# Attention in a TensorE-bound encoder: from a looped order to one straight order by heads, with maxima reduced in pairs

## The chip, the cores and the metric

The kernel runs on one core of a Trainium2 chip. TensorE does the matrix products, VectorE (DVE) and ScalarE (ACT) work on their results in PSUM, GpSimd (POOL) works on tiles in SBUF, and SyncE (SP) issues the DMAs. The engines run side by side and wait for each other through semaphores. The metric is the time on the device in microseconds, median of three runs.

## The reference

A two-layer encoder is applied to two groups of tokens, 2048 "prompt" tokens and 512 "sample" tokens, which attend only within their group. The change is in the attention of layer 0, 12 heads of width 96 for queries and keys and 64 for values:

```python
def one_block(qblk):
    s = jnp.einsum('bqhd,bkhd->bhqk', qblk, k, preferred_element_type=jnp.float32) * scale
    p = jax.nn.softmax(s, axis=-1)
    return jnp.einsum('bhqk,bkhd->bqhd', p.astype(v.dtype), v)
```

All numbers are float32. The rest (latents, head projections, memory attention, spatial gating, gates and output products) is the same in both kernels.

## The kernel before

Each float32 operand is kept as a high part in fp32r and a low part, and a product is made of several fp32r matmuls. The attention stage (`attention`, from line 937) works in chunks. A chunk is one head and 512 queries. A prompt chunk has 8 pairs of 128-key tiles (2048 keys), a sample chunk 2 pairs (512 keys). There are 48 prompt chunks and 12 sample chunks, all prompt chunks first.

For each pair t of a chunk the engines do this:

- TensorE, `scores`: six matmuls of 512 columns (two key tiles, three products each) into `sc[t % 2]`, two PSUM banks. It needs the remainder of pair t-2 (`p_lo`), which is read from the same banks, and for t = 0 the row of negated maxima of the chunk, which rides along as the 97th row of the query tile.
- ScalarE, `exps`: exp of the scores into `ph` (fp32r, L1193), and again in place (L1194).
- VectorE, `low_of`: the remainder `pl` = exact minus rounded (L1301).
- TensorE, `value`: four matmuls with `ph` and `pl` into `o_hi` and `o_lo`, two pairs behind the scores.
- GpSimd: the running sum `acc` of `ph` (L1267).
- TensorE, `maximum`, and VectorE, `maxima`: a rough product of queries and keys for a chunk further on, 16 pieces a prompt chunk, 4 a sample chunk, two pieces in each unit. A piece is one matmul into one bank (`mxp0` or `mxp1`) and one reduction by VectorE (L1287). When all pieces of a chunk are there, VectorE reduces them to four columns (`m4`, L1290) and negates them (`neg`, L1295), and SyncE copies them by four small DMAs into the query tile (`row`, L1036).

What TensorE and VectorE do for one t is called a unit here: in a full one 12 matmuls. At a chunk's end come: ScalarE's copies of the upper half and the low rows (`upper`), VectorE's `halves` (L1306, one per chunk), GpSimd's `fold`, `total_lo` and `join`, and two TensorE matmuls for the sum (`total`). The last two value products of a chunk are issued in unit 0 of the next one (`finish_values`).

The order on each engine is that of the code. `run_chunks` writes 8 chunks out, then a hardware loop of 4 passes over 8 chunks, then the other 20 chunks written out. In unit t TensorE's `step` does scores t+1, the maxima, the scores 0 of the next chunk where t is the last, then the value products. The maxima of a prompt chunk are made from 10 units ahead (`max_pieces`), those of a sample chunk two short chunks ahead.

Of the kernel before, what the change touches and what calls it, by code (L numbers as in the profile page):

```python
# [6 lines left out]
ALU = mybir.AluOpType  # L7
# [865 lines left out]
class Chunk:  # L873
# [3 lines left out]
    PROMPTS, LAST = NH * PROMPT // BLK, NH * (PROMPT + SAMPLE) // BLK - 1  # L877

    def __init__(self, j, k):
        if isinstance(j, int):  # L880
            j, k = (8 * j + k) // 8, (8 * j + k) % 8
        self.j, self.k = j, k
        self.known = isinstance(j, int)
        m = 8 * j + k - self.PROMPTS if self.known else -1
        self.sample = m >= 0
        self.pairs = 2 if self.sample else 8
        self.pieces = 4 if self.sample else 16
        p = self.PROMPTS
        self.n = j * 8 + k
        self.slot = k % 2  # L890
        self.quad = k % 4
        self.part = k % 4
        self.load = j * 2 + k // 4
        self.kv = (k // 4) % 2
        self.g0 = p * 8 + 2 * m if self.sample else j * 64 + 8 * k
        self.sum0 = p * 7 + m if self.sample else j * 56 + 7 * k
        self.mx0 = p * 16 + 4 * m if self.sample else j * 128 + 16 * k
        self.g0_mod = (2 * m) % 4 if self.sample else 0
        self.half = j * 4 + k // 2
        self.tile0 = 4 * self.part if self.sample else 0  # L900
# [1375 lines left out]
```

## Time and profile before

| | |
|---|---|
| median of three runs | 3671.3 us (3663.44 to 3674.0) |
| the profiled execution | 3671.86 us, its span 3670.1 us |
| TensorE clock granted, mean | 0.946 |
| busy in the span: TensorE, VectorE, ScalarE, GpSimd | 3348.8, 2017.9, 1582.6, 1389.7 us |

The attention stage lies between about 495 us and 1810 us of the span. A timeline row has start, duration, engine, line, operation, output and inputs; `x2` merges instructions of one kind, and the bracket is the idle time before it with what ended it. In a window row the count of instructions stands in parentheses behind each engine's busy time. A chunk's period can be read from any row that comes once a chunk, as that of `halves`.

### The profile page before, as it was taken

To read this page: it belongs to the slowest core of one execution; us is meant where nothing else is said; L and a number is where in the kernel's file an instruction comes from. 1 tells how busy PE (TensorE), PEld (TensorE's weight loads), DVE (VectorE), ACT (ScalarE), POOL (GpSimd) and SP (SyncE) were. 2 spreads that over 40 slices of the span, in tenths; PEclk is the share of its full clock that TensorE was granted. 3 is DMA by queue.
4 is the path that set the end of the run, shared out by engine and by line. 5 is a ranking of instruction groups with operands and counts; after the bars stand their busy time and mean duration, and the time that the engine had idled before them with its cause. 6 is when DMAs were issued, how large, how long until landed. Compare 5 with 4: busy or idle time off the path is not lost. (4 is left out here: it accounts for less than half of the span.)

```text
span 3670.1 us, 48958 instructions
## 1 busy us (share of the span) xinstructions
PE 3348.8 (91%) x16108; PEld 2745.4 (75%) x16108; DVE 2017.9 (55%) x3007; ACT 1582.6 (43%) x2396; POOL 1389.7 (38%) x914
## 2 busy tenths in 40 slices
PE   8969969999999999998779898997999969799899
PEld 7968847776776767776578687885888858688787
DVE  4457768888887878886557333113332337622211
ACT  4446637776776767776545222002222225412100
POOL 1147838887887878887511000000000011000000
PEclk9979979999999999998889899998999979899999
DMA  7769961222122212224243897655222245398555
GB/s 279 257 232 311 315 179 40 53 51 53 32 52 52 53 47 53 53 53 97 84 169 121 253 293 241 205 186 185 87 94 94 91 157 185 121 266 238 177 187 172
DMA packets 457298, 538.22 MB, mean 147 GB/s; under 512 B 55705, under 2 KB 372505, under 8 KB 437393
## 3 DMA queue, kind: packets, MB, share of 16 engines
q1 hardware_dynamic: 457104, 535.81, 47.6%
q8 instruction: 101, 1.65, 0.2%
q14 instruction: 93, 0.75, 0.1%
HBM read 324.98 MB, written 210.61 MB: 146 GB/s over the span
## 5 line engine op out<-in xcount | busy, mean ns | idle before, releaser
L1267 POOL TENSOR_TENSOR at_acc<-at_acc,at_ph 128x1024 f32<-128x1024 f32 x288 | 690.4, 2397 | 84.6 <-ACT at_ph L1193 70.2
L1301 DVE TENSOR_TENSOR at_pl<-at_sc,at_ph 128x1024 fp32r<-128x1024 f32 x408 | 498.0, 1221 | 184.4 <-ACT at_sc L1194 162.1
L1193 ACT ACTIVATE at_ph<-at_sc 128x1024 fp32r<-128x1024 f32 x408 | 418.8, 1027 | 398.1 <-PE at_sc L1113 397.7
L1287 DVE TENSOR_REDUCE at_mx<-at_mxp 128x1 f32<-128x512 f32 x816 | 521.8, 680 | 31.7 <-PE at_mxp L1124 29.0
L1194 ACT ACTIVATE at_sc<-at_sc 128x1024 f32<-128x1024 f32 x408 | 416.3, 1020 | 0.0
L1109 PE MATMUL at_sc<-at_qt,at_kt 97*128 97x512 f32 x816 | 337.7, 414 | 53.4 <-DMA at_qt<-at_neg 26.0
L1111 PE MATMUL at_sc<-at_qt,at_kt 96*128 96x512 f32 x816 | 330.1, 405 | 0.0
L1113 PE MATMUL at_sc<-at_qt,at_kt 96*128 96x512 f32 x816 | 329.1, 403 | 0.0
L1138 PE MATMUL at_o_hi<-at_ph,at_v 128*128 128x512 f32 x816 | 325.0, 398 | 1.5 <-DVE at_half L1306 1.5
L1140 PE MATMUL at_o_lo<-at_pl,at_v 128*97 128x512 f32 x816 | 323.4, 396 | 0.0
L1124 PE MATMUL at_mxp<-at_kt,at_qt 96*128 96x512 f32 x816 | 279.5, 415 | 29.6 <-DMA at_kt<-kT 23.0
L165 PE MATMUL ga_acc<-ga_h,ga_g_hi 128*128 128x512 f32 x640 | 256.8, 401 | 29.2 <-DMA ga_h<-hT 27.1
L165 PE MATMUL ou_acc<-ou_o_hi,ou_o 128*128 128x512 f32 x640 | 250.8, 392 | 26.2 <-DMA ou_o<-ogT 26.2
L1931 DVE TENSOR_TENSOR ou_y<-ou_acc,ou_x 128x1024 f32<-128x1024 f32 x40 | 49.0, 1224 | 381.4 <-PE ou_acc L167 381.4
L166 PE MATMUL ga_acc<-ga_h,ga_g_hi 128*128 128x512 f32 x640 | 254.0, 397 | 0.0
L167 PE MATMUL ga_acc<-ga_h,ga_g_lo 128*128 128x512 f32 x640 | 253.7, 396 | 0.0
L166 PE MATMUL ou_acc<-ou_o_lo,ou_o 128*128 128x512 f32 x640 | 250.4, 391 | 0.0
L167 PE MATMUL ou_acc<-ou_o_hi,ou_o 128*128 128x512 f32 x640 | 250.3, 391 | 0.0
L1109 PEld LDWEIGHTS at_sc<-at_qt,at_kt 97*128 97x128 f32 x816 | 156.9, 192 | 123.8 <-DVE at_pl L1301 31.3
L1124 PEld LDWEIGHTS at_mxp<-at_kt,at_qt 96*128 96x128 f32 x816 | 157.3, 193 | 96.4 <-DVE at_mx L1287 40.6
L253 POOL TENSOR_TENSOR sg_n_mse<-sg_n_ms,all_eps 128x1 f32<-128x1 f32 x24 | 5.0, 209 | 560.4 <-ACT sg_n_junk L245 560.4
L1267 POOL TENSOR_TENSOR at_acc<-at_ph 128x1024 f32<-128x1024 f32 x60 | 143.8, 2397 | 170.9 <-ACT at_ph L1193 170.8
(246 smaller groups left out, 7412.3 us busy)
## 6 DMA issues: line engine op xcount, KB each, us to landing
ma_h<-hT SPq DMA_DIRECT2D x40, 1024.0 KB, 4.8
ogT<-ga_st SPq DMA_DIRECT2D x160, 256.0 KB, 3.5
ou_o<-ogT SPq DMA_DIRECT2D x40, 1024.0 KB, 6.1
ga_h<-hT SPq DMA_DIRECT2D x64, 512.0 KB, 7.3
hT<-lat_n_h SPq DMA_DIRECT2D x24, 1024.0 KB, 6.3
hT<-sg_n_h SPq DMA_DIRECT2D x24, 1024.0 KB, 3.8
qT<-hd_stq SPq DMA_DIRECT2D x60, 384.0 KB, 6.0
kT<-hd_stk SPq DMA_DIRECT2D x120, 192.0 KB, 3.5
```

The lines of the kernel that those rows point to most:

```text
L165: pe.matmul(out, a_hi, w_hi, start=first, stop=False)
L166: pe.matmul(out, a_hi, w_lo, start=False, stop=False)
L167: return pe.matmul(out, a_lo, w_hi, start=False, stop=last)
L1109: pe.matmul(sc[g][:, b, :], kt[:, c.kv, 0, ks], qt[:, c.quad, 0, :], start=True, stop=False)
L1111: pe.matmul(sc[g][:, b, :], kt[0:QK, c.kv, 0, ks], qt[0:QK, c.quad, 1, :], start=False, stop=False)
L1113: m = pe.matmul(sc[g][:, b, :], kt[0:QK, c.kv, 1, ks], qt[0:QK, c.quad, 0, :], start=False, stop=True)
L1124: pe.matmul(mxp[n % 2][:], qt[0:QK, c.quad, 0, qn * P:(qn + 1) * P], kt[0:QK, c.kv, 0, kb * BLK:(kb + 1) * BLK], start=True, stop=True).th ...
L1193: act.activation(ph[:, g], sc[g % 2][:], ACT.Exp, scale=SCALE).then_inc(p_hi, 1)
L1194: act.activation(sc[g % 2][:], sc[g % 2][:], ACT.Exp, scale=SCALE).then_inc(p_in, 1)
L1267: pool.tensor_tensor(acc[:, c.slot, :], f32(ph[:, (g - 1) % 4]).rearrange("p b n -> p (b n)") if t == 1 else acc[:, c.slot, :], now, ALU.a ...
L1287: dve.tensor_reduce(mx[:, n:n + 1], mxp[n % 2][:], AX.X, ALU.max).then_inc(mx_in, 1)
L1301: dve.tensor_tensor(pl[:, g], sc[g % 2][:], f32(ph[:, g]), ALU.subtract).then_inc(p_lo, 1)
```

## The change

All 60 chunks are written out straight, without a hardware loop, in the order of the heads: four prompt chunks of a head and then its sample chunk. A head's keys and values are loaded whole, for both groups, the keys' high and low part by a DMA each with a semaphore of its own. The maxima run a fixed 11 units (22 pieces) ahead over all chunk boundaries. Two maximum matmuls write the two banks of one tile `mxp`, and one reduction takes both. The next pair may be written only when that reduction is done. For the first pieces, when the score buffers are still empty, `sc` serves as a ring. In a unit TensorE now does scores, value products, maxima. On the other engines the order within a unit is the same. `unit` and `free_of_sum` only find the semaphore values.

```diff
-    PROMPTS, LAST = NH * PROMPT // BLK, NH * (PROMPT + SAMPLE) // BLK - 1
-
-    def __init__(self, j, k):
-        if isinstance(j, int):
-            j, k = (8 * j + k) // 8, (8 * j + k) % 8
-        self.j, self.k = j, k
-        self.known = isinstance(j, int)
-        m = 8 * j + k - self.PROMPTS if self.known else -1
-        self.sample = m >= 0
+    PARTS = TOK // BLK
+    COUNT = NH * PARTS
+    UNITS, ADDS, PIECES = 34, 29, 68
+    LEAD = 22
...
+        self.slot, self.quad, self.kv = n % 2, n % 4, self.head % 2
+        self.half, self.turn = n // 2, n // 4
+        self.g0 = self.head * self.UNITS + 8 * self.part
+        self.sum0 = self.head * self.ADDS + 7 * self.part
+        self.mx0 = self.head * self.PIECES + 16 * self.part
+        self.tile0 = PT_TILES if self.sample else 0
...
+def unit(g):
+
+    head, rest = g // Chunk.UNITS, g % Chunk.UNITS
+    c = Chunk(head * Chunk.PARTS + min(rest // 8, Chunk.PARTS - 1))
+    return c, g - c.g0
 
 
 def run_chunks(eng, step):
 
-    for k in range(8):
-        step(Chunk(0, k))
-    with eng.Fori(1, Chunk.PROMPTS // 8 - 1) as j:
-        for k in range(8):
-            step(Chunk(j, k))
-    for n in range(Chunk.PROMPTS - 8, Chunk.LAST + 1):
-        step(Chunk(0, n))
+    for n in range(Chunk.COUNT):
+        step(Chunk(n))
...
-    if c.pairs == 2:
-        ahead, pieces = c.ahead(2), (2 * t, 2 * t + 1)
-    elif t < 5:
-        ahead, pieces = c.ahead(1), (2 * t + 6, 2 * t + 7)
-    else:
-        ahead, pieces = c.ahead(2), (2 * t - 10, 2 * t - 9)
-    return ahead, [n for n in pieces if ahead.exists() and n < ahead.pieces]
+    at = 2 * (c.g0 + t) + Chunk.LEAD
+    head, rest = at // Chunk.PIECES, at % Chunk.PIECES
+    ahead = Chunk(head * Chunk.PARTS + min(rest // 16, Chunk.PARTS - 1))
+    return ahead, [at - ahead.mx0, at - ahead.mx0 + 1] if ahead.exists() else []
...
-        kt = s.sb("kt", [QK + 1, 2, 2, PROMPT], F32R)
+        kt = s.sb("kt", [QK + 1, 2, 2, TOK], F32R)
         qt = s.sb("qt", [QK + 1, 4, 2, BLK], F32R)
-        v = s.sb("v", [P, 2, 16, VR + 1], F32R)
+        v = s.sb("v", [P, 2, TILES, VR + 1], F32R)
...
-        mxp = [s.ps(f"mxp{u}", [P, BLK]) for u in range(2)]
+        mxp = s.ps("mxp", [P, 2, BLK])
...
+        def max_buffer(pair):
+
+            return sc[pair % 2] if pair < 8 or pair == 9 else mxp
+
+        def max_free(pair):
+
+            return pair - 1 if pair < 8 else {8: 0, 9: 8, 10: 9}.get(pair, pair)
...
+                def load_k(head):
+                    for a, sem in ((0, kh_load), (1, kl_load)):
+                        sp.dma_start(f32(kt[0:QK, head % 2, a]), kT[a, head * QK:(head + 1) * QK, :]
+                                     ).then_inc(sem[head % 2], 16)
+
+                def load_v(head):
+                    sp.dma_start(f32(v[:, head % 2, :, 0:2 * VH]),
+                                 vS[:, head * (2 * VH):(head + 1) * (2 * VH)].rearrange("(t p) n -> p t n", p=P)
+                                 ).then_inc(v_load[head % 2], 16)
...
-                load_k(0, 0)
+                load_k(0)
                 load_q(c0.ahead(1))
-                load_v(0, 0)
+                load_v(0)
                 load_q(c0.ahead(2))
-                load_k(1, 1)
-                load_v(1, 1)
-                sp.wait_ge(const_in, 4)
+                load_k(1)
+                load_v(1)
+                sp.wait_ge(const_in, 5)
...
-                    more = not c.known or (c.load >= 1 and c.load + 1 < SLOTS)
-                    if c.part == 0 and more:
+                    if c.part == 0 and 1 <= c.head < NH - 1:
                         sp.wait_ge(scored, c.g0)
-                        load_k(c.load + 1, 1 - c.kv)
-                    if c.part == 1 and more:
-                        sp.wait_ge(valued, prev.g0)
-                        load_v(c.load + 1, 1 - c.kv)
-                    if c.sample and nxt.exists():
+                        load_k(c.head + 1)
+                    if c.part == 1 and 1 <= c.head < NH - 1:
+                        sp.wait_ge(valued, c.head * c.UNITS)
+                        load_v(c.head + 1)
+                    early = c.sample or nxt.sample
+                    if early and nxt.exists():
                         row(nxt)
                     if has_before(c):
-                        store(prev)
-                    if not c.sample and nxt.exists():
+                        store(before(c, 1))
+                    if not early and nxt.exists():
                         row(nxt)
...
-                    g = (c.g0_mod + t) % 2
+                        if c.part == 0:
+                            pe.wait_ge(kl_load[c.kv], loaded(c))
+                    g = (c.g0 + t) % 2
+                    if c.n == 0 and t < 2:
+                        pe.wait_ge(mx_in, 7 if t == 0 else 10)
                     after(pe, p_lo, c.g0 + (t - 1))
...
                     for n in pieces:
                         if n == 0:
-                            pe.wait_ge(q_load[c.quad], c.load * 16 + 16)
-                            pe.wait_ge(k_load[c.kv], loaded(c, 2))
-                        after(pe, mx_in, c.mx0 + (n - 1))
+                            pe.wait_ge(q_load[c.quad], c.turn * 16 + 16)
+                            pe.wait_ge(kh_load[c.kv], loaded(c))
+                        pair = (c.mx0 + n) // 2
+                        if n % 2 == 0:
+                            after(pe, mx_in, max_free(pair))
                         qn, kb = (n, c.part) if c.sample else (n // 4, n % 4)
-                        pe.matmul(mxp[n % 2][:], qt[0:QK, c.quad, 0, qn * P:(qn + 1) * P],
-                                  kt[0:QK, c.kv, 0, kb * BLK:(kb + 1) * BLK], start=True,
-                                  stop=True).then_inc(mx_mm, 1)
+                        m = pe.matmul(max_buffer(pair)[:, n % 2], qt[0:QK, c.quad, 0, qn * P:(qn + 1) * P],
+                                      kt[0:QK, c.kv, 0, kb * BLK:(kb + 1) * BLK], start=True, stop=True)
+                        if n % 2 == 1:
+                            m.then_inc(mx_mm, 1)
...
                     for t in range(c.pairs):
                         if t < c.pairs - 1:
                             scores(c, t + 1)
-                        maximum(*max_pieces(c, t))
                         if nxt.exists() and t == c.pairs - 1:
                             scores(nxt, 0)
                         if t == 0 and has_before(c):
                            value(c, t - 2)
                        if t == 3 and has_before(c):
                            total(prev)
+                        maximum(*max_pieces(c, t))
...
             def _(dve):
                 def maxima(c, pieces):
-                    for n in pieces:
-                        dve.wait_ge(mx_mm, c.mx0 + (n + 1))
-                        dve.tensor_reduce(mx[:, n:n + 1], mxp[n % 2][:], AX.X, ALU.max).then_inc(mx_in, 1)
+                    for n in pieces[::2]:
+                        dve.wait_ge(mx_mm, (c.mx0 + n) // 2 + 1)
+                        dve.tensor_reduce(mx[:, n:n + 2], max_buffer((c.mx0 + n) // 2)[:], AX.X, ALU.max).then_inc(mx_in, 1)
                     if len(pieces) and pieces[-1] == c.pieces - 1:
-                        dve.wait_ge(mx_in, c.mx0 + c.pieces)
+                        dve.wait_ge(mx_in, (c.mx0 + c.pieces) // 2)
```

TensorE, unit 0 of the second chunk, before: the end of scores 1, the two maximum matmuls, the eight value matmuls left from the first chunk, the first of scores 2.

```order
L1113 MATMUL at_sc1<-at_qt,at_kt 128x512
L1124 MATMUL at_mxp0<-at_kt,at_qt 128x512
L1124 MATMUL at_mxp1<-at_kt,at_qt 128x512
L1138 MATMUL at_o_hi<-at_ph,at_v 128x512
L1140 MATMUL at_o_lo<-at_pl,at_v 97x512
L1138 MATMUL at_o_hi<-at_ph,at_v 128x512
L1140 MATMUL at_o_lo<-at_pl,at_v 97x512
L1138 MATMUL at_o_hi<-at_ph,at_v 128x512
L1140 MATMUL at_o_lo<-at_pl,at_v 97x512
L1138 MATMUL at_o_hi<-at_ph,at_v 128x512
L1140 MATMUL at_o_lo<-at_pl,at_v 97x512
L1109 MATMUL at_sc0<-at_qt,at_kt 128x512
```

TensorE, the same unit in the changed kernel:

```order
L1091 MATMUL at_sc1<-at_qt,at_kt 128x512
L1119 MATMUL at_o_hi<-at_ph,at_v 128x512
L1121 MATMUL at_o_lo<-at_pl,at_v 97x512
L1119 MATMUL at_o_hi<-at_ph,at_v 128x512
L1121 MATMUL at_o_lo<-at_pl,at_v 97x512
L1119 MATMUL at_o_hi<-at_ph,at_v 128x512
L1121 MATMUL at_o_lo<-at_pl,at_v 97x512
L1119 MATMUL at_o_hi<-at_ph,at_v 128x512
L1121 MATMUL at_o_lo<-at_pl,at_v 97x512
L1104 MATMUL at_mxp<-at_kt,at_qt 128x512 x2
L1087 MATMUL at_sc0<-at_qt,at_kt 128x512
```

The two maximum matmuls stood ahead of the eight value matmuls and stand behind them now, right ahead of the next scores.

VectorE, units 3 and 4 of the same chunk, before (`at_pl` is the remainder, `at_m4` and `at_neg` the four maxima and their negation):

```order
L1301 TENSOR_TENSOR at_pl<-at_sc1,at_ph 128x1024
L1287 TENSOR_REDUCE at_mx<-at_mxp0 128x1
L1287 TENSOR_REDUCE at_mx<-at_mxp1 128x1
L1301 TENSOR_TENSOR at_pl<-at_sc0,at_ph 128x1024
L1287 TENSOR_REDUCE at_mx<-at_mxp0 128x1
L1287 TENSOR_REDUCE at_mx<-at_mxp1 128x1
L1290 TENSOR_REDUCE at_m4<-at_mx 128x4
L1295 TENSOR_SCALAR at_neg<-at_m4 128x4
L1301 TENSOR_TENSOR at_pl<-at_sc1,at_ph 128x1024
```

VectorE, the same place in the changed kernel:

```order
L1282 TENSOR_TENSOR at_pl<-at_sc1,at_ph 128x1024
L1268 TENSOR_REDUCE at_mx<-at_mxp 128x2
L1282 TENSOR_TENSOR at_pl<-at_sc0,at_ph 128x1024
L1268 TENSOR_REDUCE at_mx<-at_mxp 128x2
L1271 TENSOR_REDUCE at_m4<-at_mx 128x4
L1276 TENSOR_SCALAR at_neg<-at_m4 128x4
L1282 TENSOR_TENSOR at_pl<-at_sc1,at_ph 128x1024
```

The reductions of one piece each have become one of two pieces. Their place between the remainders, and that of the negation ahead of a remainder, is the same.

SyncE's issues at the start of the stage, before (down to the first row copies):

```order
L1007 DMA at_qt<-qT 96x2x512
L1018 DMA at_kt<-kT 96x2x2048
L1007 DMA at_qt<-qT 96x2x512
L1029 DMA at_v<-vS 128x16x128
L1007 DMA at_qt<-qT 96x2x512
L1018 DMA at_kt<-kT 96x2x2048
L1029 DMA at_v<-vS 128x16x128
L1036 DMA at_qt<-at_neg 1x128x1 x4
```

And in the changed kernel:

```order
L1000 DMA at_qt<-qT 96x2x512
L1006 DMA at_kt<-kT 96x2560 x2
L1000 DMA at_qt<-qT 96x2x512
L1010 DMA at_v<-vS 128x20x128
L1000 DMA at_qt<-qT 96x2x512
L1006 DMA at_kt<-kT 96x2560 x2
L1010 DMA at_v<-vS 128x20x128
L1017 DMA at_qt<-at_neg 1x128x1 x4
```

The key load is two DMAs, keys and values have 2560 tokens in place of 2048, and all of them stand ahead of the first row copies as before.

## Rows read from the trace of the kernel before

**Rows 1.** Windows: us, busy us (instructions) by engine, clock, DMA share, GB/s.

```profile
core 0: us, PE busy (x) PEld busy (x) DVE busy (x) ACT busy (x) POOL busy (x), PEclk, DMA share, GB/s
498.00:522.00 24.00, 11.96 (x18) 5.10 (x18) 13.93 (x24) 0.00 (x0) 0.00 (x0) 0.50 1.07 242
1540.00:1640.00 100.00, 99.57 (x420) 76.37 (x419) 88.85 (x117) 72.74 (x81) 87.83 (x44) 1.00 0.22 50
```

**Rows 2.** Groups, attention stage: count, busy us, mean ns, idle before and its releasers.

```profile
L1109 PE MATMUL at_sc<-at_qt,at_kt 97*128 97x512 f32 x816 | 337.7, 414 | 53.4 <-DMA at_qt<-at_neg 26.0 <-issue 19.9 <-DVE at_pl L1301 3.7
```

**Rows 3.** Timeline, VectorE's halves: start us, us, instruction, [idle before <-releaser].

```profile
581.79 0.67 DVE L1306 TENSOR_TENSOR at_half<-at_o_hi,at_up 64x512 f32<-64x512 f32 x1
...
605.24 0.67 DVE L1306 TENSOR_TENSOR at_half<-at_o_hi,at_up 64x512 f32<-64x512 f32 x1
...
888.24 0.67 DVE L1306 TENSOR_TENSOR at_half<-at_o_hi,at_up 64x512 f32<-64x512 f32 x1
...
921.74 0.68 DVE L1306 TENSOR_TENSOR at_half<-at_o_hi,at_up 64x512 f32<-64x512 f32 x1 [1.24 <-ACT at_up L1202]
...
1693.45 0.67 DVE L1306 TENSOR_TENSOR at_half<-at_o_hi,at_up 64x512 f32<-64x512 f32 x1
...
1804.95 0.68 DVE L1306 TENSOR_TENSOR at_half<-at_o_hi,at_up 64x512 f32<-64x512 f32 x1 [4.12 <-ACT at_up L1202]
```

**Rows 4.** Timeline around a chunk boundary in straight code, all engines.

```profile
580.80 0.40 PE L1109 MATMUL at_sc<-at_qt,at_kt 97*128 97x512 f32 x1
...
582.20 0.62 PE L1124 MATMUL at_mxp<-at_kt,at_qt 96*128 96x512 f32 x2
...
582.40 1.02 ACT L1193 ACTIVATE at_ph<-at_sc 128x1024 fp32r<-128x1024 f32 x1 [0.20 <-PE at_sc L1113]
...
584.37 1.22 DVE L1301 TENSOR_TENSOR at_pl<-at_sc,at_ph 128x1024 fp32r<-128x1024 f32 x1 [0.45 <-ACT at_sc L1194]
...
585.51 1.28 DVE L1287 TENSOR_REDUCE at_mx<-at_mxp 128x1 f32<-128x512 f32 x2
...
585.65 0.50 PE L1109 MATMUL at_sc<-at_qt,at_kt 97*128 97x512 f32 x1
...
590.40 0.63 PE L1124 MATMUL at_mxp<-at_kt,at_qt 96*128 96x512 f32 x2
...
590.84 1.29 DVE L1287 TENSOR_REDUCE at_mx<-at_mxp 128x1 f32<-128x512 f32 x2 [0.28 <-PE at_mxp L1124]
```

**Rows 5.** Timeline, VectorE's negation beside GpSimd, and the wait behind it.

```profile
543.84 2.38 POOL L1267 TENSOR_TENSOR at_acc<-at_acc,at_ph 128x1024 f32<-128x1024 f32 x1 [0.39 <-ACT at_ph L1193]
...
544.57 1.68 DVE L1295 TENSOR_SCALAR at_neg<-at_m 128x4 fp32r<-128x4 f32 x1
...
546.16 1.21 DVE L1301 TENSOR_TENSOR at_pl<-at_sc,at_ph 128x1024 fp32r<-128x1024 f32 x1
...
547.43 0.50 PE L1109 MATMUL at_sc<-at_qt,at_kt 97*128 97x512 f32 x1 [0.54 <-DVE at_pl L1301]
...
567.39 1.29 DVE L1287 TENSOR_REDUCE at_mx<-at_mxp 128x1 f32<-128x512 f32 x2 [0.28 <-PE at_mxp L1124]
...
568.92 0.78 DVE L1295 TENSOR_SCALAR at_neg<-at_m 128x4 fp32r<-128x4 f32 x1
```

**Rows 6.** Timeline, GpSimd after that same boundary.

```profile
583.50 2.39 POOL L1267 TENSOR_TENSOR at_acc<-at_acc,at_ph 128x1024 f32<-128x1024 f32 x1 [1.32 <-ACT at_ph L1193]
...
590.72 4.94 POOL L1267 TENSOR_TENSOR at_acc<-at_acc,at_ph 128x1024 f32<-128x1024 f32 x2
```

**Rows 7.** Timeline, start of the attention stage.

```profile
508.27 1.19 PE L1124 MATMUL at_mxp<-at_kt,at_qt 96*128 96x512 f32 x2 [23.04 <-DMA at_kt<-kT]
...
526.90 0.79 PE L1109 MATMUL at_sc<-at_qt,at_kt 97*128 97x512 f32 x1 [1.42 <-DMA at_qt<-at_neg]
```

**Rows 8.** Timeline, a row copy issued behind a key load.

```profile
1687.48 2.43 SPq L1036 DMA_DIRECT2D at_qt<-at_neg  x4
...
1696.26 0.79 PE L1109 MATMUL at_sc<-at_qt,at_kt 97*128 97x512 f32 x1 [3.16 <-DMA at_qt<-at_neg]
```

More of the change, by code:

```diff
@@ L898, in __init__ @@
-        self.g0_mod = (2 * m) % 4 if self.sample else 0
-        self.half = j * 4 + k // 2
-        self.tile0 = 4 * self.part if self.sample else 0
+        self.slot, self.quad, self.kv = n % 2, n % 4, self.head % 2
[4 more added lines that the diff above has]
+        self.tile0 = PT_TILES if self.sample else 0
+        self.after_sample = n > 0 and self.part == 0
@@ L969, in attention @@
         q_load = [s.sem(f"q_load{u}") for u in range(4)]
-        k_load = [s.sem(f"k_load{u}") for u in range(2)]
+        kh_load = [s.sem(f"kh_load{u}") for u in range(2)]
+        kl_load = [s.sem(f"kl_load{u}") for u in range(2)]
         v_load = [s.sem(f"v_load{u}") for u in range(2)]
@@ L973, in attention, with loaded @@
         o_out = [s.sem(f"o_out{u}") for u in range(2)]
-        SLOTS = NH + NH * SAMPLE // PROMPT
-        def loaded(c, parts):
-            if not c.sample:
-                return c.j * 16 + 16
-            return NH // 2 * 16 + ((c.load - NH) // 2 + 1) * 16 * parts
+        def loaded(c):
+            return (c.head // 2 + 1) * 16
         def stored(c):
@@ L1021, in load_v @@
[L1021 to L1031 removed]
+                    sp.dma_start(f32(qt[0:QK, c.quad]),
+                                 qT[c.head, :, :, c.part * BLK:(c.part + 1) * BLK].rearrange("a d t -> d a t")
+                                 ).then_inc(q_load[c.quad], 16)
@@ L1040, in sum_rows @@
                 def sum_rows(c, which):
-                    if c.sample:
-                        h = c.n - c.PROMPTS
-                        return sums_out[which, h:h + 1, PROMPT:TOK]
-                    return sums_out[which, bass.ds(c.load, 1), c.part * BLK:(c.part + 1) * BLK]
+                    return sums_out[which, c.head:c.head + 1, c.part * BLK:(c.part + 1) * BLK]
                 def store(c):
@@ L1150, in total @@
                     m.then_inc(tot_mm, 1)
-                pe.wait_ge(const_in, 4)
-                c0 = Chunk(0, 0)
+                pe.wait_ge(const_in, 5)
+                c0 = Chunk(0)
                 maximum(c0, range(c0.pieces))
-                maximum(c0.ahead(1), range(6))
+                maximum(c0.ahead(1), range(Chunk.LEAD - 16))
                 scores(c0, 0)
@@ L1312, in _ @@
                 dve.memset(f32(pick[:, ROW_HI:ROW_HI + 1]), 1.0).then_inc(const_in, 1)
-                maxima(Chunk(0, 0), range(16))
-                maxima(Chunk(0, 1), range(6))
+                maxima(Chunk(0), range(16))
+                maxima(Chunk(1), range(Chunk.LEAD - 16))
                 def step(c):
@@ L1323, in _ @@
                 run_chunks(dve, step)
-                halves(Chunk(0, Chunk.LAST))
+                halves(Chunk(Chunk.COUNT - 1))
 class MemoryRows:
```

93 lines of the change are left out of this document (27 added, 66 removed).

## The prediction

> **What bounds the kernel now.** I read the windows first. In the stretch of straight attention code TensorE issues 420 matmuls in 100 us at clock 1.00, while VectorE and GpSimd are each busy 88 us [rows 1]: TensorE is the bound there, with two engines close behind it. The timeline gives its pace: six score matmuls start in 1.40 us, 0.233 each [rows 4]. A prompt chunk is 98 matmuls (48 scores, 32 value, 16 maximum, 2 for the total), 22.8 us, and takes 23.45 [rows 3]. So a chunk has 0.6 us of stalls and no more. The scores group is one of six of 816 matmuls [rows 2]; with the 120 of the totals attention has 5,016.
>
> The idle time lies elsewhere. The halves, one a chunk, are a clock for progress. Over the loop's jump back they stand 33.50 us apart in place of 23.45 [rows 3]; the idle time put down to "issue" is 19.9 us [rows 2], in three places, and about as much again is given to the cold clock and refilling: 29 us in all. The twelve sample chunks take 111.5 us (1693.45 to 1804.95) for 12 x 26 matmuls, 72.7 us: 39 us lost, most of it the waits for the row of negated maxima, 26.0 us [rows 2, 3].
>
> From the first scores to the last value products the stage takes 526.90 to 1804, 1277 us [rows 3, 7]. Of it 4,992 matmuls x 0.233 are 1163.
>
> **What the change removes.** The jumps (29 us). The loop's address code: some 0.15 us a chunk over 32 chunks, 5 us. The sample tail (39 us): a sample chunk now stands between prompt chunks, and its row is ready many units before its scores. The small stalls of a chunk, 0.6 us, go too, but only to make room for others. If that were all, attention would shorten by over 70 us.
>
> **What it adds, in a full unit.** The maximum matmuls now stand last in a unit, two banks are reduced by one instruction, and VectorE's order is as before: remainder of scores t, then the reduction of unit t, then remainder t+1. TensorE may write scores t+3 only when remainder t+1 is done. Links of the chain, all from [rows 4]: maximum matmul to reduction 0.44, for a pair one matmul later, 0.67. The pair's reduction reads 1024 elements a partition, as the remainder does, so I take the remainder's pace of 1.14 (584.37 to 585.51). Two single ones in a row take 1.28, so the bounds are 1.06 and 1.36. Remainder to scores 1.28. Sum 3.09 us from the first maximum matmul. TensorE reaches those scores 14 matmuls after it, 3.26 us. Slack 0.17: nothing is lost, but before, with the maxima four matmuls earlier, there was about 0.9 us more.
>
> **At a chunk's start.** Unit 0 has the previous chunk's eight value matmuls, now ahead of its maxima; unit 1 has no value products. From unit 0's maxima to scores 3 are only 10 matmuls (its own two, scores 2, unit 1's maxima), 2.33 us, against the chain of 3.09. Stall 0.76, and scores that come late show 0.50 in place of 0.40 for the first matmul [rows 4], so 0.86. This holds at prompt and sample boundaries alike (between sample and prompt 18 matmuls stand where 16 do, ahead of the maxima, not behind). 57 of 59 boundaries still have maxima: 49 us.
>
> **At the negation.** Once a chunk VectorE also reduces the maxima to four and negates them: from the start of the two reductions to the negation 1.53 us, 1.46 with a pair, the negation 0.78, and the remainder starts 0.09 before its end [rows 5]. The chain is 0.67 + 1.46 + 0.78 - 0.09 + 1.28 = 4.10 against 3.26: 0.84, with the late start 0.94 a chunk. Before, the earlier maxima covered it.
>
> **The negation's own length.** It is 0.78 us in one row and 1.68 in the other. In the second it starts at 544.57 and ends at 546.25, where GpSimd's addition (543.84 + 2.38 = 546.22) ends; TensorE's scores then waited 0.54 [rows 5]. In each of some two dozen that I looked at with GpSimd at work, the negation ended with a GpSimd instruction. So its length is set by GpSimd's phase. That phase in the changed kernel, with the start of scores 2 as zero: first exponential 1.60, addition 1.10 later (582.40 to 583.50), and 7.22 us of additions, remainder of the total and join until the fourth addition (583.50 to 590.72) [rows 4, 6]. It starts at 9.9; the fifth runs from 12.4 to 14.8. TensorE: scores 3 at 2.62 (the stall above), scores 4 at 5.52, scores 5 at 8.78 (the total's two matmuls lie between), the maxima behind them at 11.1, the negation at 11.1 + 0.67 + 1.46 = 13.2. It falls well inside the fifth addition and ends with it at 14.8: 1.6 in place of 0.78, so the stall is 0.94 + 0.84 = 1.78. Three chunks of each head negate there: 36 x 1.78 = 64 us. The other two (for the sample chunk and for the next head) negate two units later; the same working gives 0.8 and 1.2: 23 x 1.0 = 23.
>
> The Trainium skill, SBUF — State Buffer, section Who interferes with whom, says that VectorE and GpSimd share a port pair as an exclusive lock, that a tensor_scalar can need it and a tensor_reduce on trn2 never does. By that rule the pair's reduction doesn't wait for GpSimd and the negation does; the trace agrees (1.68 against 0.78). It speaks against this change, since with it the wait lies on TensorE's path.
>
> **The start.** The first maxima start at 508.27, the first scores 18.6 us later [rows 7]. One pair per reduction and two score buffers as a ring save some 2 us, and waiting for only the high half of the keys some 3. Against it: ahead of the first row copy stand 7,552 KB of loads, before 6,272. At 242 GB/s [rows 1] that is 5.4 us more, and a row copy issued behind a key load landed only 8.8 us after its issue (1687.48 to 1696.26) [rows 8]. Bounds -5 and +5.4. I take +3, since the loads end after the row is ready by 10 us or more, which is the case of rows 8.
>
> **Sum.** 1163 matmuls, 3 for the cold start, 4 for the tail (4.12 of idle time at 1804.95 [rows 3]), 49 for the boundaries, 64 + 23 for negations: 1306 us against 1277, +29. With the start +3: +32. The profiled execution took 3671.9 (span 3670.1), 0.6 over the median: 3704. The other stages are untouched; neither DMA totals nor ScalarE's work changes.
>
> **Rivals.** *TensorE stays the bound, faster.* If the reductions don't hold up the scores (the chain shorter by some 0.8 us, or a cover that I overlook at the boundaries), 1163 + 7 + 60 x 0.6 = 1206, with +3 at the start 3604. For it: in the trace it is at 1.00 clock and 99.6 us of 100 [rows 1]. Against it: the four links are measured. It decides from the point where the boundary stall goes. Chance 0.13.
>
> *The negation stays at 0.78, no change.* If GpSimd's phase falls otherwise by 0.85 us, each of 59 costs 0.94, 55 in place of 87: 3672. For it: phases are the least sure numbers here. Against it: 0.8 us is large beside the errors of the links. Chance 0.17.
>
> *Full units stall too, slower still.* If the pair's reduction takes 1.36, each full unit is 0.05 over its slack and pays 0.05 + 0.10: 280 x 0.15 = 42, and 116 stalls grow by 0.22, 26: 3772. For it: 0.17 is little. Against it: VectorE's rows of 512 and 1024 elements differ by their length alone. Chance 0.12.
>
> **How the numbers follow.** The forecast has 0.58. Its own range, from errors of 0.15 us in each of 118 stalls and the start's bounds, is 3685 to 3724. About 0.3% (11 us) is what a measurement tells from no change. Slower by more: 0.54 of the forecast's 0.58, the last rival's 0.12, 0.03 of the unchanged negation: 0.69. Faster: 0.13 and 0.02: 0.15. The same: 0.16. The range leaves out the fast rival and the upper part of the slow one: 3660 to 3750.
>
> **What would show it.** Steps right: halves 25.3 to 25.7 us apart in a head's prompt chunks; scores waiting for VectorE's remainder twice a chunk, about 0.8 at the start and 1.7 late; the negation at about 1.6 us; no idle time by issue, no wait for the row copies except at the start; pair reductions of 1.2 us. Wrong: negations of 0.8 or less with halves 24.6 apart (the second rival), halves under 23.5 (the first), or waits of 0.05 to 0.2 in every unit (the third). If the row copies land after the scores want them, the estimate is short: half a microsecond in each of 48 chunks would be 24 us.

## The result and the profile after

| | before | after |
|---|---|---|
| median, us | 3672.6 (3663.4 to 3674.0, 4 runs) | 3715.5 (3708.3 to 3725.9, 4 runs) |
| profiled execution: time, span | 3671.9, 3670.1 | 3708.3, 3706.3 |
| mean granted clock | 0.946 | 0.953 |

The ratio is 1.0124 (95% interval 1.0095 to 1.0154): the changed kernel is slower by 42.9 us by the medians, and by 36.4 in the profiled executions. The forecast was 3704, slower, with a range of 3660 to 3750. The loops' idle time is gone and so is the tail of sample chunks, and TensorE still does less per microsecond.

Windows and groups of the attention stage after the change (columns as in [rows 1, 2]):

```profile
core 0: us, PE busy (x) PEld busy (x) DVE busy (x) ACT busy (x) POOL busy (x), PEclk, DMA share, GB/s
540.00:640.00 100.00, 93.27 (x389) 69.76 (x387) 82.32 (x78) 68.44 (x77) 80.02 (x39) 1.00 0.09 21
```

```profile
L1268 DVE TENSOR_REDUCE at_mx<-at_mxp 128x2 f32<-128x1024 f32 x399 | 486.5, 1219 | 229.2 <-PE at_mxp L1104 229.2
L1087 PE MATMUL at_sc<-at_qt,at_kt 97*128 97x512 f32 x816 | 340.7, 418 | 107.4 <-DVE at_pl L1282 93.7 <-DMA at_qt<-at_neg 13.6
```

In 100 us TensorE issues 389 matmuls; before it was 420 [rows 1]. Its idle time "by issue" (19.9 us) is gone and waiting for row copies now costs 13.6 in place of 26.0, but waiting for VectorE's remainders costs 93.7 in place of 3.7 [rows 2]. VectorE itself waits 229 us for maximum matmuls, so it isn't short of time. Each engine waits for the other in turn, which is a chain and not a full engine.

The timeline of one prompt chunk after the change (start us, us, engine, line, instruction, [idle before <-releaser]) shows both waits, one at each end:

```profile
563.05 0.67 DVE L1287 TENSOR_TENSOR at_half<-at_o_hi,at_up 64x512 f32<-64x512 f32 x1
...
563.19 0.50 PE L1087 MATMUL at_sc<-at_qt,at_kt 97*128 97x512 f32 x1 [0.40 <-DVE at_pl L1282]
...
570.50 7.46 POOL L1248 TENSOR_TENSOR at_acc<-at_acc,at_ph 128x1024 f32<-128x1024 f32 x3
...
573.87 1.61 DVE L1276 TENSOR_SCALAR at_neg<-at_m 128x4 fp32r<-128x4 f32 x1
...
575.39 1.21 DVE L1282 TENSOR_TENSOR at_pl<-at_sc,at_ph 128x1024 fp32r<-128x1024 f32 x1
...
576.65 0.50 PE L1087 MATMUL at_sc<-at_qt,at_kt 97*128 97x512 f32 x1 [1.50 <-DVE at_pl L1282]
...
586.27 1.23 DVE L1268 TENSOR_REDUCE at_mx<-at_mxp 128x2 f32<-128x1024 f32 x1 [1.37 <-PE at_mxp L1104]
...
587.41 1.22 DVE L1282 TENSOR_TENSOR at_pl<-at_sc,at_ph 128x1024 fp32r<-128x1024 f32 x1
...
587.55 0.73 PE L1104 MATMUL at_mxp<-at_kt,at_qt 96*128 96x512 f32 x2
...
588.54 0.67 DVE L1287 TENSOR_TENSOR at_half<-at_o_hi,at_up 64x512 f32<-64x512 f32 x1
...
588.69 0.50 PE L1087 MATMUL at_sc<-at_qt,at_kt 97*128 97x512 f32 x1 [0.40 <-DVE at_pl L1282]
```

The halves stand 25.49 us apart, before 23.45 [rows 3]. A reader of the "idle" figures alone would undercount: a matmul's end is modelled, so take the time from start to start instead. From the two maximum matmuls at 587.55 to the scores at 588.69 are 1.14 us, where two matmuls at the pace of 0.233 take 0.47, so 0.67 is lost. The pair itself started 0.08 late (it waited for the reduction before it), and the matmul behind the first score matmul comes 0.11 late. Together that is 0.86 at the chunk's start. By the same count the late wait costs 1.66 + 0.11 = 1.77 us. 98 matmuls are 22.8, and 22.8 + 0.86 + 1.77 = 25.43. The negation at 573.87 ends with GpSimd's second addition of the three (570.50 + 2 x 2.49 = 575.48).

The start, the first scores and the stage's last half after the change. The first row is SyncE's first load of the stage; SPq marks a DMA issue, and its duration is the time of issuing:

```profile
492.44 0.35 SPq L1000 DMA_DIRECT2D at_qt<-qT  x1
...
502.22 2.04 PE L1104 MATMUL at_sc<-at_kt,at_qt 96*128 96x512 f32 x4 [19.26 <-DMA at_kt<-kT]
...
513.92 13.15 SPq L1017 DMA_DIRECT2D at_qt<-at_neg  x4
...
529.30 0.80 PE L1087 MATMUL at_sc<-at_qt,at_kt 97*128 97x512 f32 x1 [13.07 <-DMA at_qt<-at_neg]
...
1844.69 0.68 DVE L1287 TENSOR_TENSOR at_half<-at_o_hi,at_up 64x512 f32<-64x512 f32 x1 [4.90 <-ACT at_up L1183]
```

The same places before the change, beside [rows 7]:

```profile
495.58 0.35 SPq L1007 DMA_DIRECT2D at_qt<-qT  x1
...
521.91 2.98 SPq L1036 DMA_DIRECT2D at_qt<-at_neg  x4
```

The first maximum matmul started 6.05 us earlier than in [rows 7] and the first row of maxima could be copied 8.0 us earlier (513.92 against 521.91). Yet the scores started 2.4 us later, since the row copy took 13.15 us merely to be issued, where it had taken 2.98. SyncE also began its loads 3.1 us earlier here (492.44 against 495.58). Counted from the first load to the first scores the start takes 36.9 us in place of 31.3, 5.5 more.

### The profile page after: what moved, and what is told of

Same layout as the page of the kernel before. It is cut to its first block and busy times, and to the rows that moved or that the text cites. A ratio compares the mean times of both kernels' runs of the same rounds, so it can differ in the third digit from the quotient of the medians.

```text
span 3706.3 us, 45708 instructions
## 1 busy us (share of the span) xinstructions
PE 3343.8 (90%) x16108; PEld 2723.9 (73%) x16108; DVE 2019.3 (54%) x2599; ACT 1588.7 (43%) x2396; POOL 1386.9 (37%) x914
## 5 line engine op out<-in xcount | busy, mean ns | idle before, releaser
L1268 DVE TENSOR_REDUCE at_mx<-at_mxp 128x2 f32<-128x1024 f32 x399 | 486.5, 1219 | 229.2 <-PE at_mxp L1104 229.2
L1087 PE MATMUL at_sc<-at_qt,at_kt 97*128 97x512 f32 x816 | 340.7, 418 | 107.4 <-DVE at_pl L1282 93.7
L1089 PE MATMUL at_sc<-at_qt,at_kt 96*128 96x512 f32 x816 | 324.9, 398 | 0.0
L1091 PE MATMUL at_sc<-at_qt,at_kt 96*128 96x512 f32 x816 | 323.7, 397 | 0.0
L1104 PE MATMUL at_mxp<-at_kt,at_qt 96*128 96x512 f32 x798 | 259.9, 407 | 0.3 <-DVE at_mx L1268 0.3
L165 PE MATMUL sg_acc<-sg_uv_hi,sg_n_h 128*128 128x512 f32 x480 | 194.5, 405 | 1.8 <-ACT sg_uv L2035 1.2
```

Source lines behind the costliest of these rows:

```text
L165: pe.matmul(out, a_hi, w_hi, start=first, stop=False)
L1087: pe.matmul(sc[g][:, b, :], kt[:, c.kv, 0, ks], qt[:, c.quad, 0, :], start=True, stop=False)
L1089: pe.matmul(sc[g][:, b, :], kt[0:QK, c.kv, 0, ks], qt[0:QK, c.quad, 1, :], start=False, stop=False)
L1091: m = pe.matmul(sc[g][:, b, :], kt[0:QK, c.kv, 1, ks], qt[0:QK, c.quad, 0, :], start=False, stop=True)
L1268: dve.tensor_reduce(mx[:, n:n + 2], max_buffer((c.mx0 + n) // 2)[:], AX.X, ALU.max).then_inc(mx_in, 1)
```

## The experiments

Eleven edited kernels ran, and the changed kernel once more (number 9). Times are medians; the kernel before had 3670 to 3672 us beside each. Differences from the changed kernel are taken from its median of 3715.5; number 9 has 3708.4 for it, so each of them can be 7 us off. The theory: the maximum matmuls, put last in a unit, start a chain (maxima, reduction, negation, remainder, scores) that is longer than the work TensorE has behind them, and GpSimd stretches the negation in it.

**1. Order of TensorE's queue alone**, in the changed kernel:

```
                             scores(c, t + 1)
+                        maximum(*max_pieces(c, t))
                         if nxt.exists() and t == c.pairs - 1:
...
-                        maximum(*max_pieces(c, t))
```

> One edit in the changed kernel: in every unit the two maximum matmuls stand again right behind the next scores, ahead of the value products (the order of the kernel before); the straight order by heads, the paired reduction and all else stay. Theory (the order of TensorE's queue makes both stalls): the chain maximum, reduction, (negation), remainder, scores gets about 0.9 us back, so the wait at a chunk's start goes and the one behind the negation falls from 1.5 to 0 to 0.5 us; chunks of 23.2 to 23.6 us in place of 25.5, TensorE's wait for remainders from 94 us to under 20, time 3605 to 3630. Rival (pairing, with its single pair of banks, is the cost): the maximum matmuls then wait for the reduction before, in most units, and the time stays over 3680.

Measured: 3611.3 us, ratio to before 0.9835 (0.982 to 0.9849). So one line moved back takes off 104 us, and the rest of the change is worth 59 us to the good. Its groups:

```profile
L1087 PE MATMUL at_sc<-at_qt,at_kt 97*128 97x512 f32 x816 | 330.4, 405 | 15.2 <-DMA at_qt<-at_neg 13.2 <-DVE at_pl L1282 1.9
L1104 PE MATMUL at_mxp<-at_kt,at_qt 96*128 96x512 f32 x798 | 258.8, 405 | 20.1 <-DVE at_mx L1268 20.1
```

The wait for remainders fell from 93.7 to 1.9 us. The rival has a small part of the truth: the maximum matmuls now wait 20.1 us for the single pair of banks, about 0.4 us once a prompt chunk. These chunks are 23.77 us.

**2. The same order in the kernel before** (loops and single maxima kept, maxima last):

> The kernel before (loops, single maxima, its own staging) with one edit: the two maximum matmuls stand last in each unit. Theory (the order alone makes the stalls, pairing is nearly neutral: 0.44 + 1.28 + 1.28 = 3.00 us of chain in place of 3.09): each of the 48 prompt chunks pays about 0.77 us at its start and 0.8 to 1.6 behind the negation, in place of its 0.6 us of small stalls: 50 to 90 us slower than before, 3720 to 3765, chunks of 24.8 to 25.5 us in place of 23.45. Rival (the pairing and its late first reduction are what hurts): under 3690, chunks under 23.9 us.

Measured: 3832.7 us, ratio 1.0437 (1.0416 to 1.0457). The direction and the cause hold: with single maxima the order alone does the harm, so pairing isn't the culprit. The size was far too small, by 68 to 113 us. Some chunks take 25.5 us, as forecast, and more take 27.0, with the same waits of about 1.6 us in both. The difference is the clock, in three neighbouring stretches of one 26.99 chunk:

```profile
core 0: us, PE busy (x) PEld busy (x) DVE busy (x) ACT busy (x) POOL busy (x), PEclk, DMA share, GB/s
597.00:600.00 3.00, 1.41 (x6) 0.85 (x5) 3.00 (x4) 1.43 (x2) 2.86 (x2) 1.00 0.03 0
600.00:603.00 3.00, 3.00 (x9) 2.27 (x8) 1.71 (x2) 1.24 (x2) 0.87 (x2) 0.54 0.17 11
603.00:606.00 3.00, 3.00 (x14) 2.33 (x13) 2.14 (x3) 1.21 (x2) 2.92 (x2) 0.89 0.38 121
```

TensorE waited (1.59 us, at 599.43), then ran some 3 us at 0.5, the level of 1.2 GHz. Up to the last prompt chunk there are 41 such slow spells, three of them at the loop's jumps. The other 38 and the stalls give nearly the whole loss: 48 x 2.0 + 38 x 1.5 = 153 us of 161.

**3. The boundary alone**: in unit 0 the maxima ahead of the previous chunk's value products, elsewhere last.

```
+                        if t == 0:
+                            maximum(*max_pieces(c, t))
                         if t == 0 and has_before(c):
                             finish_values(prev)
...
+                        if t > 0:
+                            maximum(*max_pieces(c, t))
```

> One edit in the changed kernel: in unit 0 of each chunk alone the two maximum matmuls stand ahead of the previous chunk's eight value matmuls; in all other units they stay last. Theory (the boundary stall is a term of its own, 57 times 0.86 us by the prediction): the wait of scores 3 goes, the wait behind the negation stays at about 1.5 us if GpSimd's phase moves with TensorE's, 40 to 49 us less, 3666 to 3675. Rival (the later stall swallows it: GpSimd's additions don't come earlier by as much, so the negation, which ends with GpSimd's addition, is longer by what was saved): negations of 2.0 to 2.4 us, late waits of 2.2 us or more, and a gain of only 49 less 36 x 0.8 = 20 us, about 3695.

Measured: 3759.9 us, ratio 1.0239 (1.0226 to 1.0252), 44 us slower than the changed kernel where both theories had a gain. Its timeline:

```profile
574.63 7.43 POOL L1251 TENSOR_TENSOR at_acc<-at_acc,at_ph 128x1024 f32<-128x1024 f32 x3
...
577.37 2.21 DVE L1279 TENSOR_SCALAR at_neg<-at_m 128x4 fp32r<-128x4 f32 x1
...
580.76 0.50 PE L1087 MATMUL at_sc<-at_qt,at_kt 97*128 97x512 f32 x1 [2.11 <-DVE at_pl L1285]
```

```profile
576.00:580.00 4.00, 2.65 (x12) 1.78 (x10) 3.93 (x4) 2.40 (x3) 3.71 (x3) 1.00 0.12 28
580.00:582.00 2.00, 1.24 (x5) 1.06 (x6) 2.00 (x3) 0.00 (x0) 2.00 (x1) 1.00 0.08 1
582.00:584.00 2.00, 2.00 (x7) 1.49 (x6) 0.96 (x1) 1.53 (x2) 0.49 (x2) 0.67 0.36 36
584.00:586.00 2.00, 2.00 (x6) 1.56 (x5) 1.28 (x2) 0.41 (x1) 1.94 (x1) 0.50 0.49 161
```

The rival's mechanism is there: TensorE reached the negation sooner, GpSimd didn't, and the negation again ended with GpSimd's addition (574.63 + 2 x 2.48 = 579.59), now 2.21 us long. What neither theory had is the clock: the wait of 2.11 us is followed by a spell at half speed. It costs 0.33 x 2 + 0.50 x 2 = 1.7 us. The stage has 35 such spells, three of them twice as long. This chunk takes 27.23 us.

**4. The negation's kind**, everything else as changed:

```
-dve.memset(f32(kt[QK:QK + 1, :, 0, :]), 1.0)
+dve.memset(f32(kt[QK:QK + 1, :, 0, :]), -1.0)
...
-dve.tensor_scalar(neg[:, c.slot, :], m4[:], -1.0, None, ALU.mult)
+dve.tensor_reduce(neg[:, c.slot, :], m4[:].rearrange("p (q n) -> p q n", q=4), AX.X, ALU.max)
```

> In the changed kernel the negation is a copy by tensor_reduce (maximum over one element) in place of a tensor_scalar by -1, with the same operands, place and waits; the keys' row of ones is -1 in exchange. Theory (the negation waits for GpSimd because of its kind, as by the exclusive lock): its length falls from 1.6 us to 0.1 to 0.3, TensorE's late wait from 1.5 to under 0.5 in each of 36 chunks, and the 23 later ones lose most of 0.7 to 1.1 us: 55 to 72 us less, 3643 to 3660. Rival (any short instruction of VectorE is held up at that place, or its length is not what TensorE waits for): length and waits as before, time within 10 us of 3715.

Measured: 3643.5 us, 72 under the changed kernel, ratio to before 0.9924 (0.9911 to 0.9937).

```profile
567.92 7.49 POOL L1248 TENSOR_TENSOR at_acc<-at_acc,at_ph 128x1024 f32<-128x1024 f32 x3
...
571.27 0.16 DVE L1276 TENSOR_REDUCE at_neg<-at_m 128x4 fp32r<-128x4 f32 x1
...
571.93 0.63 PE L1104 MATMUL at_mxp<-at_kt,at_qt 96*128 96x512 f32 x2
...
572.63 0.50 PE L1087 MATMUL at_sc<-at_qt,at_kt 97*128 97x512 f32 x1
```

The copy starts and ends in the middle of GpSimd's second addition (570.42 to 572.91) and takes 0.16 us. Whether VectorE waits for GpSimd is a matter of the instruction's kind, as the Trainium skill has it (SBUF — State Buffer, Who interferes with whom); the trace agrees, 0.16 us against 1.61 at the same place. Chunks are 24.05 us.

**5. GpSimd's phase.** The join, 1.25 us, was moved from behind the addition of unit 3 to behind that of unit 5:

> The changed kernel with GpSimd's join of the previous chunk's output (1.25 us) put behind its addition of unit 5 in place of unit 3; TensorE's, VectorE's and ScalarE's orders and all else are as in the changed kernel. Theory (the negation ends where GpSimd's instruction ends, so its length is GpSimd's phase): the addition that overlaps it begins at the end of the exponential, 572.04 in the changed kernel's trace, and not at 572.9, and ends 1.0 us sooner relative to the negation's start: the negation takes 0.5 to 0.7 us in place of 1.6, TensorE's late wait 0.4 to 0.6 in place of 1.5, 36 times about 1.0 us, 3672 to 3685. Rival (its length is not GpSimd's doing): 1.6 us and 3715.

Measured: 3759.9 us, ratio 1.0238 (1.0221 to 1.0256). The forecast of the time failed, that of the mechanism didn't:

```profile
574.33 2.39 POOL L1248 TENSOR_TENSOR at_acc<-at_acc,at_ph 128x1024 f32<-128x1024 f32 x1 [0.29 <-ACT at_ph L1174]
...
576.09 0.66 DVE L1276 TENSOR_SCALAR at_neg<-at_m 128x4 fp32r<-128x4 f32 x1
...
577.93 0.50 PE L1087 MATMUL at_sc<-at_qt,at_kt 97*128 97x512 f32 x1 [0.54 <-DVE at_pl L1282]
...
577.98 0.53 SPq L1032 DMA_DIRECT2D omix<-at_ost  x1
...
578.56 2.53 SPq L1017 DMA_DIRECT2D at_qt<-at_neg  x4
...
582.56 0.50 PE L1087 MATMUL at_sc<-at_qt,at_kt 97*128 97x512 f32 x1 [1.57 <-DMA at_qt<-at_neg]
```

The negation fell to 0.66 us and again ends with GpSimd's addition (576.72). But SyncE stores the joined output before it copies the row: the later join held up the store, the store held up the row, and TensorE waited for rows 36 times, 71.4 us in all (12.3 of it at the start as ever), 15 of them with a slow spell beside or behind. With the row ahead of the stores in SyncE's queue (`early = True`):

> As the kernel with GpSimd's join behind the addition of unit 5, and in SyncE's queue the row copy of the next chunk stands ahead of the stores in every chunk. Theory: there the negation did fall to 0.66 us and the late wait to 0.54, but the store waited for the later join and held up the row copy behind it (issued at 578.56, wanted at 581), 35 waits of up to 1.6 us and a slower clock behind them; with the row first only the gain is left, 36 times 0.96 us: 3675 to 3685, chunks of 24.5 us, no wait for rows but the first. Rival (the later join itself costs TensorE time): 3700 or more.

Measured: 3676.8 us, ratio 1.0013 (1.0004 to 1.0022), chunks of 24.55, no slow spell.

```profile
575.79 0.66 DVE L1276 TENSOR_SCALAR at_neg<-at_m 128x4 fp32r<-128x4 f32 x1
...
577.63 0.50 PE L1087 MATMUL at_sc<-at_qt,at_kt 97*128 97x512 f32 x1 [0.54 <-DVE at_pl L1282]
```

So 39 of the 43 us are gone by shifting one GpSimd instruction and one queue entry.

**6. Both stalls treated**: unit 0 as in 3, the negation as in 4.

> The changed kernel with both edits: maxima ahead of the value products in unit 0 alone, and the negation as a copy by tensor_reduce with keys' row -1. Theory (unit 0's edit does take away the boundary stall; alone it lost time because the negation then fell to 2.2 us, TensorE waited 2.1 us and the granted clock fell to 0.5 for 3 us behind it): the gain now shows, 57 times 0.75 to 0.86 us below 3643.5, so 3593 to 3602, clock 1.00 throughout, chunks of 23.2 to 23.4 us. Rival (the moved maxima themselves cost the time): 3650 or more.

Measured: 3609.7 us, 34 under number 4, not 42 to 49; clock 1.00. The chunks are 23.62 us, 0.43 shorter, and 34 us over the 57 boundaries are 0.6 each. So unit 0's edit does help, by half to two thirds of the boundary's 0.86 us. What is left of it comes from another chain:

```profile
562.70 1.23 DVE L1271 TENSOR_REDUCE at_mx<-at_mxp 128x2 f32<-128x1024 f32 x1 [0.54 <-PE at_mxp L1104]
...
564.21 1.23 DVE L1286 TENSOR_TENSOR at_pl<-at_sc,at_ph 128x1024 fp32r<-128x1024 f32 x1 [0.29 <-ACT at_sc L1178]
...
564.84 0.63 PE L1104 MATMUL at_mxp<-at_kt,at_qt 96*128 96x512 f32 x2
...
565.49 0.50 PE L1087 MATMUL at_sc<-at_qt,at_kt 97*128 97x512 f32 x1
```

Scores 4 start at 565.49, where two matmuls behind 564.84 they were due at 565.31, and the matmul behind them comes another 0.11 late. They waited for remainder 2. That one didn't wait for the reduction, which had ended at 563.93, but 0.29 us for ScalarE's second exponential of scores 2. Unit 1 has no value products, so TensorE is soon back here too.

**7. What a longer wait costs.** One more reduction of 512 elements (0.67 us) behind each negation of the changed kernel:

> The changed kernel with one more tensor_reduce of 512 elements a partition (0.5 to 0.65 us, its result unused) behind each negation. Two theories of what a stall costs. First (TensorE's clock: a wait of some 2 us is followed by about 3 us at 0.5 to 0.67 of the clock, 1.7 us lost, as where the negation took 2.2 us; one of 1.5 us is not): the late wait goes from 1.50 to about 2.1, and each of the 36 chunks pays 0.6 + 1.7 us, the 23 other negations 0.6: 3800 to 3820, mean clock below 0.945. Second (a wait costs its own length, no more): 59 times 0.6, 3745 to 3752, clock as in the changed kernel.

Measured: 3803.2 us, ratio 1.037 (1.0354 to 1.0387), mean clock 0.936, as the first theory had it. It is 88 us more, for 59 x 0.6 = 35 us of added waiting by the forecast. The profiles are 93.5 us apart. TensorE's waits for remainders grew by 29.5 us of that (123.2 in place of 93.7). The other 64 go with the clock: 35 slow spells, seven of them twice as long, with 72 us of clock missing in them, where the changed kernel's profile has two spells and 3 us. But not each wait of 2.06 us has a spell behind it, and some of 1.55 have:

```profile
579.10 0.50 PE L1089 MATMUL at_sc<-at_qt,at_kt 97*128 97x512 f32 x1 [2.06 <-DVE at_pl L1285]
```

From 575 to 590 the granted clock is 1.00 throughout.

**8. The start.** Head 1's loads issued behind the first row copy:

> In the changed kernel the loads of head 1's keys and values are issued behind the first row copy in place of ahead of it; nothing else. Theory (the first row copy, 13.1 us from issue to landing, waits in the queues behind those bulk loads): it lands within 3 us, the first scores start 10 to 11 us earlier relative to the first maxima, and the time falls by 9 to 11 us, to about 3705. Rival (the loads of head 0 themselves, or the bandwidth, hold it up): less than 3 us.

Measured: 3704.3 us, 11 under the changed kernel (4 under its median in number 9), ratio to before 1.0085 (1.0071 to 1.0098).

```profile
514.17 2.52 SPq L1017 DMA_DIRECT2D at_qt<-at_neg  x4
```

The issue takes 2.52 us in place of 13.15, and the first scores start at 518.74, 10.6 us earlier. The profiled span is 3708.6, though, 2.3 above the changed kernel's. The stage behind the first scores is 8.2 us longer and what follows the stage 4.7. In the stage it has 8 slow spells behind late waits of 1.46 to 1.49 us; the changed kernel's first profile has two, one in each of these windows:

```profile
1040.00:1048.00 8.00, 7.66 (x27) 5.64 (x26) 5.92 (x7) 3.88 (x4) 4.62 (x3) 0.79 0.22 49
1805.00:1810.00 5.00, 4.99 (x15) 3.85 (x16) 2.56 (x3) 1.94 (x2) 2.88 (x2) 0.66 0.08 4
```

**9. The changed kernel once more**, for what that means:

> The changed kernel itself again, unedited, for its spread and for a second profile. The kernel with the later loads of head 1 had the same late waits (1.46 to 1.49 us), but 8 spells of slow clock behind them where the first profile of the changed kernel had 1, each 1.7 us. Theory (a wait of 1.5 us leaves it open whether the clock falls, and this makes the spread from run to run): the median is again 3710 to 3722, the runs spread over 10 to 18 us, and this profile's span is 3704.6 plus 1.7 for each spell between 545 and 1800 us, within 4 us. Rival (the spread comes from other stages or the loads): the span doesn't follow the number of spells.

Measured: 3708.4 us (3705.6 to 3715.6), ratio 1.0108 (1.0091 to 1.0124), two spells, span 3704.4. As written, the forecast did poorly: its rule gave 3708.0, at the edge of its 4 us, and the median missed the bracket. But the rule counted up to 1800 us and so left out the first profile's second spell, at 1806; with two in both profiles it would give 3706.3. Take the stage alone, from the first scores to the last half. It is 1315.4 us with two spells, 1313.7 with two and 1323.6 with eight (number 8). Less 1.7 us for each spell these are 1312.0, 1310.3 and 1310.0, and the first has a wait for a row (0.56 us) that the others don't have. So within the stage the spells account for the differences to some 2 us. The rest of the spread lies outside it: what follows the last half takes 1861.6, 1860.4 and 1866.3 us in the same three profiles. The clocks of the runs without a profile point the same way. In number 8 the shortest of the six spans is 3692.7 at a mean clock of 0.956, and the two longest are 3708.3 at 0.952 and 3708.6 at 0.953. By an estimate from these rounded figures 162 us of clock are missing in the first and 178 and 174 in the others.

**10. Candidates.** Old order, no negation at all, later loads:

```
-dve.tensor_reduce(m4[:], ...)
-dve.tensor_scalar(neg[:, c.slot, :], m4[:], -1.0, None, ALU.mult)
+dve.tensor_reduce(neg[:, c.slot, :], mx[:, 0:c.pieces].rearrange("p (q n) -> p q n", q=4), AX.X, ALU.max)
```

> Candidate to beat both: the changed kernel with maxima behind the scores again in all units, no negation at all (the reduction to four maxima writes the row's source, the keys' row is -1), and head 1's loads behind the first row copy. Theory: 3611 of the old order, less 10 to 11 us at the start, less what is left of waits behind negations (chunks of 23.75 us there against 22.8 of matmuls; 0.3 to 0.6 us a chunk of it by negations, 15 to 30 us): 3572 to 3590. Rival (in that order TensorE's rest of stalls comes from the single pair of banks, not from the negation): 3597 to 3602.

Measured: 3602.7 us, ratio 0.981 (0.9794 to 0.9825). The rival was right (3597 to 3602, missed by 1). Only the start was gained; chunks stay at 23.77 us, with the wait for the pair of banks (20.1 us in all) as in number 1. The last one takes the other order (only unit 0 ahead) with the same two edits:

> Second candidate to beat both: maxima ahead of the value products in unit 0 alone and last in the others, no negation (row of maxima, keys' row -1, so also without the copy of e9_unit0_reduce), head 1's loads behind the first row copy. Theory: the chunks of 23.61 us lose the late 0.3 us behind the copy (0.2 of it), and the start gives 10 to 11 us: 3609.7 less 10.5 less 59 x 0.2 = 3585 to 3592. Rival (the late wait is not the copy's doing): 3597 to 3601.

Measured: 3591.4 us (3588.0 to 3593.6), ratio 0.9782 (0.9769 to 0.9796). That is inside the theory's 3585 to 3592. It beats both kernels, by 81 and 124 us, with chunks of 23.42.

## Why the prediction was right

The sign, the mechanism and the size of each stall were right. At the start two terms were off and made up for each other, which was luck. Point by point:

- *Pace of 0.233 and 22.8 us a chunk*: held. The forecast for a head's prompt chunks was 25.3 to 25.7. The first two intervals of a head measure 25.5, the third 26.3 and the fourth 25.0, 25.6 on the mean, since a head's negations don't fall into its chunks evenly. A whole head takes 109.20 us (halves 646.76 and 755.96) where the terms give 97.4 + 11.6 = 109.0.
- *Boundary stall 0.86*: measured 0.67 + 0.08 + 0.11 = 0.86. Partly luck in its make-up: 0.08 of it is a maximum pair that waits for the reduction before, which the prediction didn't have. Number 6 shows that moving unit 0's maxima gives back only half to two thirds of it, since a second chain, over ScalarE's exponentials, is nearly as long there.
- *Negation 1.6, stall 1.78*: measured 1.61 and 1.77. The phases, called the least sure numbers, held to 0.1 us. Numbers 4, 5 and 3 show it from three sides: another kind (0.16 us), another phase (0.66), and another (2.21). The second rival (the negation stays short) was the right counterpart: number 5's second kernel is just that case, and has 3677 where the rival's sum said 3672.
- *The later negations, 0.8 and 1.2*: losses of 0.8 and 1.3 us.
- *Full units have slack, if only 0.17*: held; scores wait for remainders 117 times, always behind a chunk's start or a negation. From the pair's reduction to the remainder behind it are 1.14 us (586.27 to 587.41), the price taken.
- *Removed: jumps 29, address code 5, tail 39*: 73 us. Number 1 is 59 under before, and its 48 prompt chunks are 0.32 us longer than before's 23.45, which is 15: 74.
- *Start +3*: +2.4 by the first scores, but not by the terms given. The maxima came 8.0 us sooner, where the working had 5: 3.1 of it because SyncE's first load was issued that much earlier, and this first issue lies between 492.4 and 498.5 us in the fourteen profiles. Between issuing the row copy and the first scores are 15.4 us in place of 5.0, 10.4 more, where the working had about 8. From the first load on the change costs 5.5 us at the start, which is the prediction's bound for the larger loads (5.4). Number 8 shows the cause: with fewer loads ahead of the row copy the first scores come 10.6 us sooner.
- *Sum +32*: the profiled executions differ by 36.4, and from the first scores to the last value products (1843.6) are 1314.3 us where 1306 was said. The small terms were short: the cold start cost 5 us and not 3, the tail 6 and not 4, each head 0.1 to 0.2 more, and two slow spells 1.7 each. Those 8 us too many are halved by luck: what follows the last half takes 3.5 us less than before (1861.6 against 1865.2), within the spread that number 9 shows for it. The prediction's own range was worked out from 118 stalls where its terms have 57 + 59 = 116, which changes nothing.

What the prediction lacked is the clock. It priced a stall at its length. The kernel lies where that is nearly true (two spells in each of its profiles, for some 36 waits of 1.5 us); had each wait been 0.6 longer, the time would have been 3803 (number 7) and outside the range. The clock is also the likely part of the median's 43 us against the profile's 36: the three other runs have a mean clock of 0.951 against the profiled 0.953, an estimated 7 us of clock missing. No trace of those runs shows it, and one of them (3725.9) is 9 us longer still at the same clock. On number 9's occasion the median was 38.5 above before.

## What to carry to other kernels

Where an engine hands work to another and must have it back, count its own instructions between the hand-over and the place that needs the answer, in every kind of unit; the order inside the unit matters most where that count is lowest (here 10 matmuls at each chunk's start, against 14 in a full unit). A tiny VectorE instruction can last as long as what GpSimd is doing; put it in a kind that doesn't wait for GpSimd (here tensor_reduce, 0.16 us) and fold the sign into a constant, here the keys' row. That was worth 72 us. Before moving one instruction, follow what its in-order queue holds behind it: the join that shortened the negation delayed a store, the store a row copy, and the gain of 39 us became a loss of 44.

When you count events in a trace, count to the end of the stage. One spell that stood 6 us behind a round limit made number 9 look like evidence against its theory.

## What was not expected of the hardware

- A short wait on TensorE can cost more than itself. Behind waits of 1.5 to 2.1 us the granted clock fell to 0.50 for about 3 us, about 1.7 us of clock missing each: 35 times in number 3, 35 in number 7, 38 in number 2. The length of the wait alone doesn't decide: with the same late waits of about 1.5 us the changed kernel had two spells in each of two profiles, and number 8, which differs at the start only, had eight; a wait of 2.06 us had none. What else decides stays open. In number 5's second kernel, with late waits of 0.54 and none above 1.1 us, there was no spell in 1250 us.
- Four tiny row copies, issued 4 us behind bulk loads in one SyncE queue, held the queue for 13.15 us; issued 12 us behind them, in the kernel before, 2.98; ahead of head 1's loads, 2.52. In the first two the issue ended at nearly the same time (527.1 and 524.9), so having the row ready earlier gained nothing.
